# A two-block fp32 kernel on one core: five edits to who does what when

## What is computed

```
# block 1
h = rmsnorm(x);  xbc, dt_raw, z_ssd, sc_h, sc_b, sc_c, z_sc = split(h @ w_in)
dt = softplus(dt_raw + dt_bias);  a = -exp(a_log)
# chunks of 128 positions, 16 heads of 64 channels in 2 groups, state of 64 per head
y = (masked decay of C B^T) @ (x dt)  +  decay * C @ state        # scan_second
state = decay * state + B^T @ (x dt decay)
x = x + sigmoid((x + rmsnorm(mix)) @ w_ple_gate) * (p @ w_ple_proj)     # PLE projection
# block 2
scores = q_t k_s exp(cum_t - cum_s), s <= t, in chunks of 64, 4 heads   # diagonal and levels
f = square(relu(h @ w_ff1)) @ w_ff2                                     # FF pairs
```

## Time and profile before

| | |
|---|---|
| median of 3 runs | 2454.61 us (2453.95 to 2457.71) |
| the profiled execution | 2452.28 us, span 2450.6 us |
| mean granted clock | 0.989 |
| TensorE busy | 2372.3 us, 97% |
| VectorE busy | 1538.1 us, 63% |
| GpSimd busy | 1165.5 us, 48% |
| ScalarE busy | 846.1 us, 35% |

### The profile page before, as it was taken

The page is one execution under the profiler, slowest core; times in us unless marked ns, Lnnn a source line. Parts: engine busy times, 40 slices in busy tenths (PEclk is TensorE's granted clock), DMA queues, the critical chain, the costliest instruction groups (busy, mean ns, idle before and its releaser), DMA issues.

```text
span 2450.6 us, 33556 instructions
## 1 busy us (share of the span) xinstructions
PE 2372.3 (97%) x12578; PEld 1931.4 (79%) x12578; DVE 1538.1 (63%) x1926; ACT 846.1 (35%) x1288; POOL 1165.5 (48%) x659
## 2 busy tenths in 40 slices
PE   7999999999999899999999999999999999999996
PEld 5777877888888688778877787788877888788885
DVE  6777878876611761113157767645798666777788
ACT  4555464432200221252023223222263333343444
POOL 4375667663434553233223323333464555566664
PEclk9999999999999999999999999999999999999998
DMA  5313333336111322122222222232134444853322
GB/s 209 129 75 137 122 125 107 133 128 242 43 51 49 122 96 70 48 104 74 85 78 82 64 77 81 66 99 83 60 121 145 162 161 142 293 225 133 130 91 81
DMA packets 126655, 277.38 MB, mean 113 GB/s; under 512 B 11713, under 2 KB 56001, under 8 KB 121938
## 3 DMA queue, kind: packets, MB, share of 16 engines
q1 hardware_dynamic: 84544, 216.04, 25.4%
q10 hardware_dynamic: 42002, 59.87, 7.1%
HBM read 199.26 MB, written 76.61 MB: 113 GB/s over the span
## 4 chain that ended last, share of the span: by engine, by line
PE 60%; DVE 9%; issue 3%; DMA 2%; ACT 2%; POOL 1%; SPq 0%; DVEq 0%; ACTq 0%; POOLq 0%
PE pt L2650 32%; PE pt L3103 14%; PE wk L3103 6%; PE pt L2666 1%; DMA eb<-o_d 1%; PE wk L3015 1%; PE wk L3114 1%; DVE darg L2190 1%; POOL xl L711 1%; DVE eb L2272 1%; PE wk L2985 1%; PE wk L3053 1%; PE wk L3048 1%; PE wk L3049 1%; PE wk L2937 0%
## 5 line engine op out<-in xcount | busy, mean ns | idle before, releaser
L676 POOL TENSOR_TENSOR w_hi<-w_raw,ones 128x1024 fp32r<-128x1024 f32 x94 | 181.9, 1935 | 752.9 <-PE pt L2650 711.2
L680 POOL TENSOR_TENSOR w_lo<-w_raw,w_hi 128x1024 fp32r<-128x1024 f32 x104 | 279.4, 2686 | 83.6 <-ACT w_hi L931 60.7
L2650 PE MATMUL pt<-h,w_hi 128*128 128x512 f32 x896 | 289.7, 405 | 1.8 <-ACT cu_o L1309 1.8
L2650 PE MATMUL pt<-l,w_hi 128*128 128x512 f32 x896 | 277.5, 391 | 0.0
L2650 PE MATMUL pt<-h,w_lo 128*128 128x512 f32 x896 | 277.1, 390 | 0.0
L2650 PEld LDWEIGHTS pt<-l,w_hi 128*128 128x128 f32 x896 | 168.8, 188 | 36.3
L2650 PEld LDWEIGHTS pt<-h,w_lo 128*128 128x128 f32 x896 | 168.6, 188 | 36.2
L2650 PEld LDWEIGHTS pt<-h,w_hi 128*128 128x128 f32 x896 | 161.1, 189 | 37.9 <-ACT ebuf L1304 5.3
L796 POOL TENSOR_TENSOR wr_l<-raw,wr_h 128x512 fp32r<-128x512 f32 x80 | 137.1, 1719 | 81.0 <-ACT wr_h L1451 81.0
L738 POOL TENSOR_TENSOR xl<-sraw,xh 128x512 fp32r<-128x512 f32 x80 | 135.8, 1707 | 83.3 <-ACT xh L998 83.3
L796 POOL TENSOR_TENSOR wr_l<-fraw,wr_h 128x512 fp32r<-128x512 f32 x60 | 79.2, 1323 | 92.6 <-ACT wr_h L1451 92.6
(11 more groups left out here) (577 smaller groups left out, 6096.3 us busy)
## 6 DMA issues: line engine op xcount, KB each, us to landing
w_raw<-ws_d SPq DMA_DIRECT2D x106, 512.0 KB, 3.3
fx_d<-stg SPq DMA_DIRECT2D x106, 256.0 KB, 2.7
sraw<-ws_d SPq DMA_DIRECT2D x32, 512.0 KB, 5.9
fraw<-ws_d SPq DMA_DIRECT2D x32, 512.0 KB, 4.8
raw<-ws_d SPq DMA_DIRECT2D x32, 512.0 KB, 9.1
xs0f<-fx_d SPq DMA_DIRECT2D x10, 1024.0 KB, 5.2
xs1f<-fx_d SPq DMA_DIRECT2D x9, 1024.0 KB, 5.0
xs2f<-fx_d SPq DMA_DIRECT2D x9, 1024.0 KB, 4.9
```

The lines of the kernel that those rows point to most:

```text
L676: nc.gpsimd.tensor_tensor(out=w_hi[:, u, :], in0=w_raw[:, u, :], in1=zeros, op=ALU.add).then_inc(w_hi_done, 1)
L680: nc.gpsimd.tensor_tensor(out=w_lo[:, u, :], in0=w_raw[:, u, :], in1=w_hi[:, u, :].bitcast(f32), op=ALU.subtract).then_inc(w_split, 1)
L2650: ins = MM(pt[:, slot, h * HALF:(h + 1) * HALF], wt[:, k * P:(k + 1) * P], x[:, k, h * HALF:(h + 1) * HALF], start=first and k == 0 and n ...
```

## The change

Five edits.

1. The two broadcasts leave ACT's list. SP issues them now, behind `weights(1, 4, 0)` and ahead of the wait for `stat_done`.
2. `first_sums(0)` stands behind product 3 of the PLE projection.
3. In `scan_second` all 16 matmuls of `xd` come first, then 16 of `state`, which take only the 64 rows of their group. So they are 64x64 tiles, of which four lie side by side, and the order of heads (0, 1, 8, 9, 2, 3, ...) gives four different ones in a row.
4. The diagonal with its two waits stands behind step 2 of product S.
5. On DVE, the low parts of T4 (`operand_rest(12)` to `(15)`) and pair 2's `out_u2` and `out_s5` come ahead of `plain_operands(0)`: two low parts, the two results, the two other low parts.

```diff
@@ SP
         weights(1, 4, 0)
+        sp.dma_start(dtb[:], dt_bias.to_broadcast([P, HEADS])).then_inc(sml_in, 16)
+        sp.dma_start(alr[:], a_log.to_broadcast([P, HEADS])).then_inc(sml_in, 16)
         sp.wait_ge(stat_done, 2)
         sc_load(0)
@@ ACT
         act.dma_start(wdt_raw[:], w_dt.rearrange("(k p) h -> p k h", p=P)).then_inc(sml_in, 16)
-        act.dma_start(dtb[:], dt_bias.to_broadcast([P, HEADS])).then_inc(sml_in, 16)
-        act.dma_start(alr[:], a_log.to_broadcast([P, HEADS])).then_inc(sml_in, 16)
@@ DVE
             operand_rest(8 + k)
+        operand_rest(12)
+        operand_rest(13)
+        dve.wait_ge(x_free, B_XFREE + 8)
+        out_u2(2)
+        out_s5(2)
+        operand_rest(14)
+        operand_rest(15)
...
         plain_operands(0)
-        for k in range(4):
-            operand_rest(12 + k)
         dve.wait_ge(tl_done, 16)
-        dve.wait_ge(x_free, B_XFREE + 8)
...
-            out_u2(n)
-            out_s5(n)
+            if n > 2:
+                out_u2(n)
+                out_s5(n)
             out_22(n)
@@ TensorE
-            if n == 2:
+            if n == 3:
                 first_sums(0)
...
+            def head(h):
+                return wka[(h % 2) * 64:(h % 2) * 64 + 64, (h // 2) * P:(h // 2 + 1) * P]
+
             for h in range(HEADS):
-                o = wka[(h % 2) * 64:(h % 2) * 64 + 64, (h // 2) * P:(h // 2 + 1) * P]
-                MM(o, xd[:, h, :], rowb[:, h, :], start=True, stop=False)
-                MM(o, state[:, h, :], ce[:, h % HG, :], start=False, stop=True)
+                MM(head(h), xd[:, h, :], rowb[:, h, :], start=h % 8 < 2, stop=False, skip_group_check=True)
+            for n in range(HG // 2):
+                for g in range(GROUPS):
+                    for h in (g * HG + 2 * n, g * HG + 2 * n + 1):
+                        MM(head(h), state[g * 64:g * 64 + 64, h, :], ce[g * 64:g * 64 + 64, h % HG, :], start=False, stop=True,
+                           skip_group_check=True)
...
                 def in_ga(k):
-                    if k == 0:
+                    if k == 2:
                         pe.wait_ge(ch_in, i * 32 + 32)
                         pe.wait_ge(gst_done, i + 1)
```

## The result

The changed kernel took 2465.07 us (median of nine runs, 2460.07 to 2468.16), the kernel before 2453.95 (nine runs, 2451.56 to 2457.71). The ratio is 1.0038, with a 95% interval of 1.0028 to 1.0048: slower by 9.3 us of 2454 (6.9 to 11.8). The ratio is taken over the runs and not from the two medians, which lie 11.1 apart. The forecast was +4.0, no change that can be measured. The time lies just inside the range, which ends at 2465.5. No measurable change had 0.51 and slower had 0.42; it came out slower.

A forecast was written before the change was run, and what follows sets the result against it. TensorE, working in 97% of the span, was taken to bound the kernel. −0.1 + 15.5 − 2.8 − 3.0 − 4.0 − 1.6 = +4.0 on 2454.6 gave 2458.6 us; 8-in-10 range 2452.5 to 2465.5.

The forecast's parts named there:

- the bound: Whole kernel: about 0.2% (4.9 us) can be told from no change; slower means above 2459.5 us.
- Broadcasts, +15.5: Before the step-size product: TensorE waits 13.2 us for the late broadcasts, and low clock behind costs 2.3.
- Rival A: Step-size product: clock stays low to its end, costing 7.0 us and not 2.3; sum +8.7, 2463.3 us; chance 0.20.
- Rival C: Behind the broadcast stall: part is absorbed, the 3.5 us wait at 141.8 goes; sum −1.4, 2453 us; chance 0.15.
- Rival D: Broadcasts: they land before 67.7 and cost nothing; sum −11.5, 2443 us; chance 0.03.
- Sums, −2.8: Start, PLE projection: first sums of squares behind product 3 fill TensorE's idle time, spread starts at about 27.6; 2.8 us saved.
- Scan, −3.0: Scan's state part: 0.62 us saved per chunk, half kept in chunks 1 to 6, all in first and last.
- Rival B: Scan's state part: four tiles don't run at once or drains eat the saving; sum +7 to +8.9, 2462 us; chance 0.15.
- Diagonal, −4.0: Gated attention, chunk 0: steps 1 and 2 fill the wait for `qkc`, level 0 then waits for `kp`; 4.0 us saved.
- FF pair 2, −1.6: FF pair 2: the 4.11 us wait for `s5` goes, a new 2.6 appears, T2 starts at 1865.2; 1.6 us saved.
- put that at 1858.1: FF pair 2: low parts, operand sums and `out_22` let the T4 product start at 1858.1, after 2.6 us idle.

The follow-up runs named there:

- the two blocks: Kernel before with all xd matmuls first, then all state matmuls, these still over 128 rows; one run, 2453.51 us.
- the other order of edit 5: Kernel before with the four operand sums first, then one low part of T4, u2 and s5, then three low parts; ratio 0.9983.
- the best kernel: Kernel before with edits 2, 3 and 4 and the other order of edit 5, broadcasts left as before; ratio 0.9951.

## Why the prediction came out as it did

The result was on the slower side of the bound, the forecast on the near side of it. That the time still lay in the range is in part luck: the terms of edits 1, 2 and 5 were too good by 5.4 us together, and that of the scan was too small by 1.7. By its steps:

1. **Broadcasts, +15.5: measured +16.3.** Right in mechanism and place. The wait was 14.4 where 13.2 was worked out. SP issued the first broadcast at 76.42, 0.9 before the 77.34 that was taken (edit 2's lead of 1.0, handed on through ScalarE and GpSimd). But the second took 4.4 us to land, so TensorE went on at 81.24 and not at 80.9, and it had arrived 1.0 earlier itself. The clock cost 1.9 (2.7 with edit 1 alone), for 2.3. Rival A, low clock through all of the product, fell: full pace was back after five of its 16 groups. Its sum, +8.7, comes close to the measured 9.3 by chance. Rival C, the absorbed stall, fell: the 3.5 us wait behind it was 3.6. (Its far end adds up to 2448.1, and not to 2449.) Rival D fell with the 14.4 us.
2. **Sums, −2.8: measured −1.0** in this pair of traces. The step that failed is the sentence that the chain "takes the same time from there". The chain runs beside GpSimd's split of the next tile, which edit 2 pulls forward since it waits for product 3. In the kernel before, that split ran beside two additions (from 29.52, 3.68 us); the prediction doesn't speak of it. And "What follows hangs on the spread's end" was wrong too: with the spread at the forecast's 27.6 and the split later, the xBC product came no sooner.
3. **Scan, −3.0: measured −4.7** (4.1 from 235 to 550, and 0.6 in chunk 0). The 0.62 per chunk was exact. The half that was taken off for chunks 1 to 6 was wrong: the chain that was to bind contained two VectorE operations (L1874) whose length hangs, through GpSimd's collision, on TensorE. The prediction named just this collision as what could come back, and gave it half. Rival B fell: the 64 records took 2.93 us. Without changes of shape the `xd` block takes 1.79 us (338.46 to 340.25 in the two blocks), and 32 records at the pace of four tiles (half of 55 ns) would make 0.87; the two changes together then cost 0.27, an estimate, where 0.24 was charged. The Trainium skill, "TensorEngine Tiling (Array Packing)", section "Key Properties", has TensorE drained at a change of tiling mode. The rows agree with that, at this small price: the `xd` block takes 1.90 where a change follows it.
4. **Diagonal, −4.0: measured −4.1** in this pair of traces. After, the rest of the wait for `qkc` is 1.12 and level 0 waits 1.39 for `kp`, as worked out. But edit 4 was never run alone, and part of the 4.1 is the kernel before's own: its wait of 3.90 was followed by a low clock that lasted longer than in six of the seven other traces without the edit. From 1230 to 1275 the five traces with edit 4 fall by 4.0 to 4.1 us against it, and the seven others without edit 4 by 0.0 to 1.9. Against the mean of all without it, the gain is 2.8. TensorE, after, to hold against the earlier trace rows:

```profile
1255.56 1.15 PE L3036 MATMUL wk<-qkc 128*128 128x128 f32 x8 [1.12 <-DMA qkc<-cu_d]
...
1259.50 0.68 PE L3026 MATMUL wk<-qc,kp 128*64 128x64 f32 x8 [1.39 <-DVE kp L2204]
```

5. **FF pair 2, −1.6: measured +1.2** (−0.1 in the run with edit 5 alone, 0.6 without edit 1). The step failed in "put that at 1858.1": it counted VectorE's work up to `out_22` and not the transfer that `out_22` waits for, though the operand sums were among what moved. VectorE's own work would have let T4 start at 1856.9 by the clock of the kernel before, 1.2 sooner than that; the put held it 2.6 longer. And the idle time that it did forecast was priced without the low clock behind it, which the prediction had counted for the waits of 9.4, 3.5 and 3.9 us. In the end the wait of 4.01 took the place of one of 4.11, and the rest is that clock, which varies: from T4 to T2 is 5.44 us at full pace, 8.46 in the changed kernel and 7.07 with edit 5 alone.

By places the five make 7.7, and 9.3 ± 2.5 is what the runs gave. The sum missed by 3.7: +1.8 of edit 2, +2.8 of edit 5, +0.8 of edit 1, −1.7 of edit 3.

These are differences to one trace of the kernel before, whose own low clock is in them. Taken between the mean of all traces that have an edit and the mean of all that don't have it (its variants left out), the five are +16.8, −1.0, −4.6, −2.8 and 0.0 (edit 5: 0.6 with it, 0.5 without), in sum +8.4, which is nearer to the 9.3. The same means give −8.4 for all but edit 1 (−9 measured) and, with −3.9 for the other order of edit 5, −12.3 for the best kernel (−12 measured). By them the diagonal, which came out right against the one trace, was 1.2 too good, and edit 5 is worth nothing rather than a loss.

## What to carry to other kernels

When a transfer is moved, look who counts its semaphore, not who reads its data: here TensorE stood 14.4 us for 16 KB that it never reads, and counting it elsewhere made the late transfer free. When work on one engine is moved, follow also what waits on the thing moved, transfers among it (a put that must land before a buffer is written again), and ask what starts earlier elsewhere and what that runs beside. A gain that is said to be swallowed by another engine's chain has to be checked at that chain's longest operations: if one is long only through a collision, its end may hang on the engine that was made faster. And what a trace of before shows behind a wait is one draw: compare several traces at a place before a figure of it is called a gain.

## What the runs showed of the hardware

- VectorE operations of 0.17 us on four columns took 1.12 and 2.25 us beside GpSimd's operations over 128x1024, and ended within 0.05 us of them. That looks like being held until it ends rather than slowed. Without GpSimd beside them they took 0.17 again. Three additions over 128x512 took 5.80 us where they collided, and 2.29 where they hardly did.
- In 64x64 tiles, 32 records of 128 columns took 1.03 us with four different tiles in a row, 1.52 with the same 64 rows in eight heads behind one another, and 1.75 over 128 rows.
- Two small broadcasts of 8 KB landed in 2.9 to 3.0 and 4.4 to 5.0 us (three executions) behind 512 KB on the same queue.
- Behind the 14.4 us wait TensorE ran at half its clock until 85.2, some 4 us, and that cost 1.9 us; behind the 4.0 us wait for `out_22`, 15 matmuls took 6.3 us at a mean clock of 0.51. The length of the wait did not set the price: 14.4 us cost 1.9 and 14.6 cost 2.7; 4.0 us cost 3.0 in one execution and 1.6 in another.
- In each execution TensorE fell to the low clock at some places that no edit touched, and not at the same ones each time. So the offset between two executions wandered by up to 9 us before 1230 (edit 5 alone, which changes nothing there). Times of single executions can't tell edits of a few us; rows at their places can, where several executions agree.
